# Two of the four low quarters of a layer norm's output made by GpSimd

## The reference

```python
for l in range(2):
    proj = x @ w_in[l]                 # layer 0: state-space mixer, layer 1: windowed attention
    mixed = concat(main, mem_out) @ w_out[l]
    x = layer_norm(ALPHA * x + mixed, ln_g[l, 0], ln_b[l, 0])     # norms 0 and 2
    ffn = peer_ffn(x, peer_wq[l], ...)                            # starts with x @ peer_wq[l]
    x = layer_norm(ALPHA * x + ffn, ln_g[l, 1], ln_b[l, 1])       # norms 1 and 3
```

## Time and profile before

| | |
|---|---|
| Median of three runs | 3396.55 us (3393.91 to 3400.82) |
| The profiled execution's own time | 3398.16 us |
| Its span in the profile | 3396.4 us |
| TensorE, matmuls busy | 3335.5 us, 98% |
| VectorE busy | 2786.8 us, 82% |
| ScalarE busy | 1927.2 us, 57% |
| GpSimd busy | 482.1 us, 14% |
| Mean granted TensorE clock | 0.989 of full |

### The profile page before, as it was taken

How to read it: one execution, slowest core, us unless ns; L and a number is a source line. 1 busy time by engine, 2 the same in 40 slices (tenths; PEclk the granted TensorE clock), 3 DMA queues, 4 the chain that set the end, 5 groups by cost and what they waited for, 6 DMA issues and landing times.

```text
span 3396.4 us, 51704 instructions
## 1 busy us (share of the span) xinstructions
PE 3335.5 (98%) x19476; PEld 3002.8 (88%) x19476; DVE 2786.8 (82%) x3851; ACT 1927.2 (57%) x3370; POOL 482.1 (14%) x264
## 2 busy tenths in 40 slices
PE   8999999999999999999998999999999999999998
PEld 7888779999999988888887877999999998888887
DVE  4664658998999978889986746999899988888897
ACT  4555445555666655555555545555666665555555
POOL 0000000011222212223300000001122221222320
PEclk9999899999999999999999989999999999999999
DMA  6553245687999989999984334578799988999995
GB/s 255 180 180 137 86 157 186 247 342 297 343 363 360 361 319 356 360 362 376 379 310 149 118 124 156 196 273 336 291 362 360 361 338 342 352 362 364 378 378 217
DMA packets 169072, 969.02 MB, mean 285 GB/s; under 512 B 18896, under 2 KB 52688, under 8 KB 55376
## 3 DMA queue, kind: packets, MB, share of 16 engines
q1 hardware_dynamic: 132048, 698.61, 55.0%
q0 software_dynamic: 36864, 268.45, 20.8%
HBM read 951.26 MB, written 15.73 MB: 285 GB/s over the span
## 4 chain that ended last, share of the span: by engine, by line
PE 94%; DVE 4%; ACT 1%; DMA 1%; issue 0%; DVEq 0%; SPq 0%; ACTq 0%
PE ps L914 93%; DVE wl L1515 1%; PE ps L1101 0%; ACT wh L529 0%; DVE arena L1674 0%; DMA arena<-in_v,idx 0%; DVE xx L1533 0%; DVE arena L1640 0%; DMA kv_scratch<-arena 0%; DVE arena L1618 0%; DVE arena L1621 0%; DVE arena L1619 0%; ACT arena L587 0%; DMA arena<-in_memT 0%; PE ps L1136 0%
## 5 line engine op out<-in xcount | busy, mean ns | idle before, releaser
L1515 DVE TENSOR_TENSOR wl<-raw,wh 128x1024 fp32r<-128x1024 f32 x1264 | 1526.2, 1221 | 487.4 <-ACT wh L529 483.8
L914 PE MATMUL ps<-xx,wh 128*128 128x384 f32 (+1 forms) x5504 | 1711.5, 373 | 16.9 <-DVE wl L1515 10.5
L529 ACT ACTIVATE wh<-raw 128x1024 fp32r<-128x1024 f32 x1264 | 1333.6, 1057 | 619.1 <-PE ps L914 514.0
L914 PE MATMUL ps<-xx,wl 128*128 128x192 f32 (+1 forms) x5504 | 1424.0, 259 | 0.0
L914 PE MATMUL ps<-wh,act 128*128 128x512 f32 x3584 | 1191.1, 390 | 3.6 <-DVE act L1538 3.5
L914 PEld LDWEIGHTS ps<-xx,wh 128*128 128x128 f32 x5504 | 1036.1, 188 | 79.6 <-DVE wl L1515 11.3
L914 PEld LDWEIGHTS ps<-xx,wl 128*128 128x128 f32 x5504 | 1052.0, 191 | 0.5
L914 PE MATMUL ps<-wl,act 128*128 128x512 f32 x2304 | 897.7, 390 | 0.0
L914 PEld LDWEIGHTS ps<-wh,act 128*128 128x128 f32 x3584 | 673.9, 188 | 146.1 <-DVE act L1538 3.5
L914 PEld LDWEIGHTS ps<-wl,act 128*128 128x128 f32 x2304 | 433.2, 188 | 89.2
L1486 POOL DMA_INDIRECT arena<-in_v,idx x128 | 266.8, 2084 | 832.5 <-DVE arena L1850 812.8
(11 more groups left out here) (212 smaller groups left out, 1723.9 us busy)
## 6 DMA issues: line engine op xcount, KB each, us to landing
raw<-in_u SPq DMA_DIRECT2D x256, 1024.0 KB, 6.5
raw<-in_v SPq DMA_DIRECT2D x256, 1024.0 KB, 7.4
raw<-in_w SPq DMA_DIRECT2D x119, 1024.0 KB, 4.8
h_scratch<-hring SPq DMA_DIRECT2D x128, 96.0 KB, 5.5
hring<-h_scratch SPq DMA_DIRECT2D x128, 96.0 KB, 7.8
arena<-in_memT SPq DMA_DIRECT2D x4, 512.0 KB, 6.6
arena<-in_xT SPq DMA_DIRECT2D x4, 512.0 KB, 7.6
arena<-in_urows,idx POOLq DMA_INDIRECT x128
```

The source lines that it names most:

```text
L529: nc.scalar.activation(wh[:, j, :], raw_piece(p), ACT.Copy).then_inc(hi_ready, 1)
L914: return nc.tensor.matmul(out, lhs, rhs, start=start, stop=stop, **kw)
L1515: v.tensor_tensor(wl[:, j, :], raw_piece(p), wh[:, j, :].bitcast(F32), ALU.subtract).then_inc(lo_ready, 1)
```

## The change

GpSimd makes low quarters 1 and 3 (the second and fourth) of norms 0, 1 and 2; VectorE makes 0 and 2. GpSimd counts `pool_low`. VectorE waits for it and then executes a copy of one column whose only use is to count `x_ready`, so that the counts still come in the order of the quarters. VectorE's order becomes: gain and shift 0 and 1, low 0, gain and shift 2, weight piece `p_next + 1`, gain and shift 3, wait and copy for quarter 1, low 2, wait and copy for quarter 3, weight piece `p_next + 2`.

```diff
+        def low_halves(n):
+            for k, q in enumerate((1, 3)):
+                part = slice(q * CQ, (q + 1) * CQ)
+                pool.wait_ge(xh_ready, QX * (n + 2) + q + 1)
+                nc.gpsimd.tensor_tensor(xl[:, part, :], xt[:, part, :], xh[:, part, :].bitcast(F32), ALU.subtract)\
+                    .then_inc(pool_low, 1)
+
+        low_halves(0)
         for layer in range(2):
             base = 2 * PAIRS * layer
+            if layer:
+                low_halves(1)
+                low_halves(2)
...
-                if n < 3 and q >= 1:
-                    low_quarter(xt, n + 2, q - 1)
+                if n < 3 and q == 1:
+                    low_quarter(xt, n + 2, 0)
                 if n < 3 and q == 2:
                     lo(p_next + 1, 1)
             if n < 3:
-                low_quarter(xt, n + 2, QX - 1)
+                dve.wait_ge(pool_low, 2 * n + 1)
+                v.tensor_copy(lnmv[:, 0, 7:8], iota[:, 0:1]).then_inc(x_ready, 1)
+                low_quarter(xt, n + 2, 2)
+                dve.wait_ge(pool_low, 2 * n + 2)
+                v.tensor_copy(lnmv[:, 1, 7:8], iota[:, 0:1]).then_inc(x_ready, 1)
                 lo(p_next + 2, 2)
```

More of the change, by code:

```diff
@@ L363, in build @@
     xn0_ready, xn1_ready = sem("xn0_ready"), sem("xn1_ready")
+    pool_low = sem("pool_low")
     xtr_ready, xta_ready = sem("xtr_ready"), sem("xta_ready")
```

## The result

The changed kernel took 3405.22 us in the median of 8 runs (3401.46 to 3409.42) against 3395.36 (3392.35 to 3400.82) for the kernel before: ratio 1.0028, 95% interval [1.0019, 1.0037], so +9.5 us, between 6.5 and 12.6. That is slower by 0.28%, and the interval reaches down to 0.19%. The profiled execution is the fastest of these runs, 3401.46 us with a span of 3399.7; single executions of one kernel differ by 8 us here, nearly as much as the effect, so I read the three hand-overs and not the span.

What follows compares the result with a forecast made beforehand. TensorE, busy 98% of the span, was taken as the bound, so only its waits at the three hand-overs count. Under full exclusion norms 0, 1 and 2 add +2.05, +1.6 and +2.2, +5.85 on 3396.55: 3402.4 us, range 3395.5 to 3407.5.

Steps and rivals of the forecast that it cites:

- D: Duration of one GpSimd subtraction of 128x1024 in norms 0 to 2: 2.3 us, with ends 1.8 and 2.7.
- Exclusion: In norms 0 to 2, VectorE operations with two SBUF inputs and GpSimd subtractions never run together: sum +5.85 us.
- The row of stretched gathers: Gathers beside VectorE's two-input operations: median 1.68 us but maximum 4.76 with the v rows, read as leaning to hindrance.
- Who comes first: GpSimd's quarter 1 subtraction or VectorE's weight piece: GpSimd in norms 0 and 2, the piece in norm 1; sum 5.3 to 6.7.
- When quarter 3 is ready: TensorE's start of the fourth input quarter under full exclusion: +2.05 us in norm 0, +1.6 in norm 1, +2.2 in norm 2.
- the free case: Rival 1, no hindrance between GpSimd and VectorE in the three norms: +1.5 us, 3398.1 us, chance 0.28.
- the second rival: TensorE's clock falls behind its idle time, or GpSimd's subtraction exceeds 2.7 us, under exclusion: +6.6 to +11 us, chance 0.15.
- Within 0.2%: Whole kernel's time changes by less than 0.2%, 6.8 us, either way: chance 0.68.
- slower: Whole kernel slower by more than 0.2%, from most of rival 2 and a third of the forecast's case: chance 0.29.

Runs made afterwards that it cites:

- e2: Kernel before, with GpSimd also subtracting quarters 1 and 3 into a scratch area nobody reads, VectorE still making all low quarters: 3409.60 us, ratio 1.0036.
- e3: Changed kernel with GpSimd's two subtractions per norm replaced by a memset of the same quarters to zero: 3393.18 us, ratio 0.9989.
- e1: Kernel before with VectorE in the changed kernel's order, making all low quarters itself without GpSimd: 3400.62 us, ratio 1.0010.
- e4: Changed kernel with 12 surplus TensorE matmuls into an unused bank ahead of input quarter 1: 3402.95 us, ratio 1.0017.
- e5: Kernel before with GpSimd making the low half of weight piece p_next + 1, VectorE making all low quarters: 3394.66 us, ratio 0.9992.
- e7: Changed kernel with weight piece p_next + 1 moved behind gain and shift 3 in VectorE's order: 3403.52 us, ratio 1.0017.
- e10: Changed kernel with only low quarter 1 on GpSimd, low 2 and 3 staying on VectorE: 3404.81 us, ratio 1.0019.

## Why the prediction was off, step by step

The measured 3405.22 us lies in the stated range of 3395.5 to 3407.5 and 2.8 us above the 3402.4; the added time was forecast at +5.85 and measured at +9.5.

- **D.** Forecast 2.3 us, measured 2.37 undisturbed. Right, though it was the middle between two ends and no row had it.
- **Exclusion.** Taken in full, for a reason that I called weak; e2 and e3 show it, in both directions and for reads only. The Trainium skill (SBUF — State Buffer, section "Who interferes with whom") states just this, and the traces agree: 3.09 us for a piece of 1.22, 3.48 us for a subtraction of 2.37, and no delay beside a memset (e3). The row of stretched gathers that I leaned on remains unexplained; nothing ran that tests it.
- **Who comes first.** GpSimd in norms 0 and 2, VectorE in norm 1, as worked out from margins of 0.34, 0.15 and 0.02 us. The 0.02 decided nothing, so norm 1 came out right by luck: there GpSimd's record starts 0.05 us ahead, and VectorE still kept its duration.
- **When quarter 3 is ready.** Norm 0: copy's end forecast at 8.64 us behind the first quarter (496.75 - 488.11), measured 492.18 - 483.71 = 8.47. Norm 1: 8.19 and 7.84. Norm 2: 8.42 and 8.63. The arithmetic of the waits held within 0.4 us.
- **The step that failed** is that TensorE would then be free. The forecast had quarters 1 and 2 done at 1.48 us each, said of the free case "so the later quarter 1 costs nothing", and left the clock to the second rival with a chance of 0.15. It fell in all three norms, behind gaps of 3.15, 2.70 and 3.32 us, and even behind the 2.36 us of e1. Quarter 3 started 0.63, 0.96 and 0.70 us behind the end of VectorE's copy that counts it, where the second rival had put 0.7 per norm; e4 against the changed kernel gives 2.95 us for all three. The rival's own sum with all three norms hit, 5.85 + 3 x 0.7 = 7.95, is the hand-overs' +7.8, and its +6.6 to +11 holds the measured +9.5, though its upper part rests on a D of 3 that did not come. The forecast's +5.85 is what e4 measured without the fall: +5.8, and +4.9 in the hand-overs. So the mechanism was right and a term was set at nothing. The argument against the fall, that 3.5 us of idle is only slightly longer than one that did it, was no argument against it at all: it speaks for it.
- **Within 0.2%** had a chance of 0.68 and did not come by the ratio (0.28%, interval 0.19 to 0.37%); slower had 0.29.
- What stays open: the 1.7 us between the three hand-overs' +7.8 and the measured +9.5. It lies within the interval, and I do not explain it. Open too is how often the fall comes: each kernel has one profiled execution, and near-equal gaps went both ways.

## What to carry to other kernels

Before GpSimd gets a share of VectorE's work, look at which operands both read at that moment: an operation on two SBUF tensors and a GpSimd subtraction run one after the other, and GpSimd's takes twice as long. Give it a piece that falls beside reads from PSUM (e5: neither engine was held, and no gain clear of the noise was measured), and compute TensorE's new idle time as well as the new ready time: a gap of 2.4 us was paid for twice, once as idle and once at half clock behind it. An order that looks free because the last quarter comes no later is free only while TensorE runs at full clock.

## What the runs showed of the hardware that was not expected

- The granted clock fell behind gaps of 2.20 (e2, norm 0), 2.25 (e7, norm 0), 2.36 (e1), 2.56 (e7, norm 1), 2.70, 3.15 and 3.32 us (the changed kernel), and did not behind one of 1.61 (before). But the length alone does not decide: gaps of 2.70 and 2.71 us brought the fall in norm 1 of the changed kernel and norm 2 of e10, one of 2.70 none in norm 1 of e10, and the clock held behind 2.17 (e7, norm 2) and 2.85 us (e2, norm 1).
- Nor does the fall begin at one distance behind the gap. In norm 0 of the changed kernel the first three chunks, about 1.15 us, still run at full clock; in norm 0 of e10 the clock is 0.50 from the first chunk on (stretch 493.0 to 495.8 us).
- An earlier start in the timeline does not say who waits. Where GpSimd's record started 0.05 or 0.06 us ahead of VectorE's (norm 1 of the changed kernel, of e2 and of e10), GpSimd waited; where it started 0.16 us ahead (norm 2 of the changed kernel), VectorE did, its piece lasting 3.29 us.
- A GpSimd subtraction that meets a chain of VectorE operations gets its turn late: two of them took 7.94 us in e2, beside a VectorE that lost 3.3. The weight piece that started 1.18 us behind GpSimd's record kept its 1.22 us, so the first of them let two VectorE operations go by; in norm 2 it let one go by (3.40 us), and the piece then took 3.40.
